# A decoder step with a mixture of experts: the expert loop written out, three places for weights, and the up-projection as three fp32r products

## The reference, cut to what matters

```
def hier_moe(x, w_rg, b_rg, w_re, b_re, w_e1, w_e3, w_e2):
    ...
    for g in range(N_GROUPS):
        a = jnp.einsum('nd,edf->nef', xf, w_e1[g])      # 1024 -> 256, per expert
        b = jnp.einsum('nd,edf->nef', xf, w_e3[g])      # 1024 -> 256, per expert
        hid = jax.nn.silu(a) * b * gates[:, g, :, None]
        y = y + jnp.einsum('nef,efd->nd', hid, w_e2[g]) # 256 -> 1024, per expert
```

## Time and profile before

| | us |
|---|---|
| median of 3 runs | 1281.07 |
| lowest and highest run | 1278.13, 1283.64 |
| span of the profiled execution, first to last instruction | 1278.4 |
| PE busy in it | 1121.3 (88%) |
| the experts, from the first gathered rows on PE to the last product | 837.1 to 1210.3 |

### The profile page before, as it was taken

One profiled execution on the slowest core, in us unless ns is written; L12 is line 12 of the kernel. 1 busy time (PEld: TensorE's weight loads), 2 busy tenths in 40 slices (PEclk: granted clock), 3 DMA queues, 4 the chain that ended last, 5 costly groups with the idle time before them and its releaser, 6 DMA issues. The chain is left out here.

```text
span 1278.4 us, 13014 instructions
## 1 busy us (share of the span) xinstructions
PE 1121.3 (88%) x4858; PEld 798.0 (62%) x4858; DVE 432.0 (34%) x993; ACT 250.8 (20%) x501; POOL 195.9 (15%) x229
## 2 busy tenths in 40 slices
PE   3999998999999999998789999279999999999800
PEld 3899997978864799855457787234444444444300
DVE  5816363055541000314521135711222221222165
ACT  4522110233220121303211033101011010110121
POOL 3301220000001221000103001412211222212100
PEclk9999999999999999999899999679999999999955
DMA  9401111231025310332061121338999999888383
GB/s 329 108 17 50 37 50 62 89 138 70 1 84 181 109 38 33 138 126 99 1 230 67 66 83 50 141 132 321 334 322 334 315 328 336 320 330 310 131 311 124
DMA packets 50743, 202.82 MB, mean 159 GB/s; under 512 B 10374, under 2 KB 19071, under 8 KB 41223
## 3 DMA queue, kind: packets, MB, share of 16 engines
q1 hardware_dynamic: 38615, 177.18, 39.4%
q0 software_dynamic: 12080, 24.98, 5.3%
HBM read 189.55 MB, written 28.36 MB: 170 GB/s over the span
## 5 line engine op out<-in xcount | busy, mean ns | idle before, releaser
L420 PE MATMUL bank<-regA_r,regW_r 128*128 128x352 f32 (+1 forms) x456 | 149.4, 328 | 0.0
L419 PE MATMUL bank<-regA_r,regW_r 128*128 128x352 f32 (+1 forms) x456 | 149.4, 328 | 0.0
L395 PE MATMUL bank<-regW,regY 128*128 128x512 f32 x256 | 114.7, 601 | 1.5 <-DVE regY L1763 1.5
L395 PE MATMUL bank<-regY 128*128 128x512 f32 x256 | 112.5, 592 | 1.5 <-DVE regY L1763 1.5
L291 POOL TENSOR_TENSOR regW_r<-regW,regW_r 128x1024 fp32r<-128x1024 f32 x19 | 47.2, 2487 | 307.7 <-ACT regW_r L285 307.7
L395 PEld LDWEIGHTS bank<-regW,regY 128*128 128x128 f32 x256 | 49.3, 193 | 64.0 <-issue 64.0
L418 PE MATMUL bank<-regY_r,regW_r 128*128 128x352 f32 (+1 forms) x264 | 88.0, 333 | 0.5 <-ACT regB L981 0.5
L395 PEld LDWEIGHTS bank<-regY 128*128 128x128 f32 x256 | 48.6, 190 | 62.4 <-issue 62.4
L419 PEld LDWEIGHTS bank<-regA_r,regW_r 128*128 128x128 f32 x456 | 86.5, 190 | 0.4
L420 PEld LDWEIGHTS bank<-regA_r,regW_r 128*128 128x128 f32 x456 | 86.0, 189 | 0.0
L1770 DVE TENSOR_TENSOR regA<-regA,bank 128x256 f32<-128x256 f32 x32 | 13.5, 421 | 213.8 <-ACT regA L1231 213.8
(11 more groups left out here) (279 smaller groups left out, 1774.9 us busy)
## 6 DMA issues: line engine op xcount, KB each, us to landing
regW<-in_we SPq DMA_DIRECT2D x16, 2048.0 KB, 9.8
regY<-in_we SPq DMA_DIRECT2D x16, 2048.0 KB, 9.2
regY<-in_we SPq DMA_DIRECT2D x16, 1024.0 KB
regW<-in_we SPq DMA_DIRECT2D x16, 1024.0 KB
regB<-expert_rows SPq DMA_DIRECT2D x12, 512.0 KB, 5.5
regW<-in_wbc SPq DMA_DIRECT2D x11, 512.0 KB, 3.5
regA<-in_kct SPq DMA_DIRECT2D x5, 1024.0 KB, 4.9
regY<-in_cache_mem_v SPq DMA_DIRECT2D x5, 1024.0 KB, 7.6
```

Of the source, the lines that this page charges most:

```text
L395: last = nc.tensor.matmul(out, lhsT, rhs, start=(k == 0), stop=(k == len(pairs) - 1))
L419: nc.tensor.matmul(out, stays[1], moves[0], start=False, stop=False)
L420: ins = nc.tensor.matmul(out, stays[0], moves[0], start=False, stop=last)
```

## The change

Five edits, all in the expert part:

1. The hardware loops over experts are gone on all engines; all 32 experts are written out. The counters of the semaphores run over all experts instead of one for each parity. On POOL the small copies of the indices ahead of each gather and scatter (`gixg`, `gixs`) and the helper `waited` are gone there; the indirect DMAs read `idx` directly, and up to four gathers are issued ahead of the first scatter instead of three.
2. The weights have three places: `regW`, `regY` and `regS`. The third is loaded for expert 2 by SP after `s_gd` (the router's last values) and after the stores of `normed_tokens`, ahead of the first gather. From then on, SP waits for `ab(e-3)` before `W13(e)` and for `yy(e-3)` before `W2(e)`.
3. `ab` is made of three fp32r products for each of the 8 blocks (low weight x high token, high weight x low token, high x high) instead of one fp32 product.
4. For this each expert's `W13` is split: ACT rounds it in 4 pieces of 128 x 1024 into `W13hi` (two places in `regB`), DVE subtracts it in 4 pieces in place. The transposed tokens are split in 2 pieces of 128 x 512 in the same way.
5. On PE the tokens of expert `e+2` are transposed where those of `e+1` were, and `xt` signals each half. Experts 0 and 1 have their weights split ahead of the loop: on ACT before the router's exponentials, on DVE after the router's last instruction.

The order on ACT for expert `e` is now: `sil(e)`, `ht(e-1)`, two pieces of `W13(e+2)`, two of the tokens of `e+2`, two more of `W13(e+2)`, `y0(e-1)`. On DVE: `hid(e)`, `xt(e+2)`, the same pieces, `y1(e-1)`.

Diff, cut to its core. The places and PE:

```
+        R13 = [(regW, regWr, 0), (regY, regYr, 0), (regS, regSr, 0)]
+        W13hi = [v3(regBr, 4096 * s, KD, 2 * FE) for s in range(2)]
...
-            def ab(s, signal, b):
-                mm_group(bank[b][:, :], [(XGT[s][:, k, :], W13[s][:, k, :]) for k in range(KD)], signal)
+            def ab(e):
+                s, w, b = e % 2, e % 3, B_AB[e % 2]
+                if e >= 2:
+                    pe.wait_ge(m_hid, e - 1)
+                for k in range(KD):
+                    if k % 4 == 0:
+                        pe.wait_ge(m_xl, 2 * e + k // 4 + 1)
+                    if k % 2 == 0:
+                        pe.wait_ge(m_wl, 4 * e + k // 2 + 1)
+                    product(bank[b][:, :], (XGThi[s][:, k, :], XGTlo[s][:, k, :]),
+                            (W13hi[s][:, k, :], W13lo[w][:, k, :]), k == 0, k == KD - 1,
+                            m_ab if k == KD - 1 else None)
...
+            def down(e):
+                pe.wait_ge(m_ht, e + 1)
+                pe.wait_ge(m_w2[e % 3], 16 * (e // 3 + 1))
+                if e >= 1:
+                    pe.wait_ge(m_yo0, e)
+                    pe.wait_ge(m_yo1, e)
+                yy(e % 2, e % 3, m_y)
+            tokens(0)
+            tokens(1)
+            for e in range(NE):
+                ab(e)
+                if e >= 1:
+                    hidden(e - 1)
+                if e + 2 < NE:
+                    tokens(e + 2)
+                if e >= 1:
+                    down(e - 1)
```

SP, whose `load` starts one DMA:

```
-            sp.wait_ge(m_ab[0], 1)
-            load(w13_flat[0], i_["we"][2, :, 0:4096], m_w[0])
-            with sp.Fori(0, NE // 2 - 2) as i:
-                for e0, s in ((1, 1), (2, 0)):
-                    sp.wait_ge(m_ab[s], i + e0)
-                    weights(w13_flat[s], 2 * i + e0 + 2, 0, 4096, m_w[s])
-                    sp.wait_ge(m_y[1 - s], i + 1)
-                    weights(w2_flat[1 - s], 2 * i + e0 + 1, 4096, 6144, m_w2[1 - s])
+            sp.wait_ge(s_gd, 1)
+            sp.wait_ge(s_xnd[0], 16 * 5)
+            sp.wait_ge(s_xnd[1], 16 * 4)
+            load(w13_flat[2], i_["we"][2, :, 0:4096], m_w[2])
+            load(w2_flat[2], i_["we"][2, :, 4096:6144], m_w2[2])
+            for e in range(3, NE):
+                sp.wait_ge(m_ab, e - 2)
+                load(w13_flat[e % 3], i_["we"][e, :, 0:4096], m_w[e % 3])
+                sp.wait_ge(m_y, e - 2)
+                load(w2_flat[e % 3], i_["we"][e, :, 4096:6144], m_w2[e % 3])
```

ACT:

```
+            for e in range(NE):
+                act.wait_ge(m_ab, e + 1)
+                sil(e % 2, B_AB[e % 2], m_sil)
+                if e >= 1:
+                    act.wait_ge(m_th, e)
+                    ht((e - 1) % 2, m_ht)
+                if e + 2 < NE:
+                    weight_hi(e + 2, 0)
+                    weight_hi(e + 2, 1)
+                    token_hi(e + 2, 0)
+                    token_hi(e + 2, 1)
+                    weight_hi(e + 2, 2)
+                    weight_hi(e + 2, 3)
+                if e >= 1:
+                    y_left(e - 1)
```

The split on DVE (the tokens' `token_hi` and `token_lo` are built alike):

```
+            def weight_lo(e, c):
+                s, w = e % 2, e % 3
+                dve.wait_ge(m_wh, 4 * e + c + 1)
+                tt(W13lo[w][:, 2 * c:2 * c + 2, :], W13[w][:, 2 * c:2 * c + 2, :],
+                   W13hi[s][:, 2 * c:2 * c + 2, :].bitcast(F32), ALU.subtract).then_inc(m_wl, 1)
```

POOL:

```
-                    g.wait_ge(m_si[s], i + 1)
-                    g.wait_ge(m_yo0[s], i + 1 + s)
-                    g.wait_ge(m_yo1[s], i + 1 + s)
-                    waited()
-                    scatter(s, gixs[s], m_sc[s])
+            for e in range(4):
+                rows_in(e)
+            for e in range(NE):
+                if e + 4 < NE:
+                    rows_in(e + 4)
+                if e >= 1:
+                    rows_out(e - 1)
```

More of the change, by code:

```diff
@@ L348, in trunk_step @@
         s_waited = sem("s_waited")
[L349 to L352, removed]
+        m_w = [sem(f"m_w{s}") for s in range(3)]
+        m_w2 = [sem(f"m_w2{s}") for s in range(3)]
         m_g = [sem("m_g0"), sem("m_g1")]
[L354 to L363, removed]
-        m_sc = [sem("m_sc0"), sem("m_sc1")]
+        m_sc = [sem("m_sc0"), sem("m_sc1")]
+        m_tx = sem("m_tx")
+        m_xt = sem("m_xt")
+        m_xh = sem("m_xh")
+        m_xl = sem("m_xl")
+        m_wh = sem("m_wh")
+        m_wl = sem("m_wl")
+        m_ab = sem("m_ab")
+        m_sil = sem("m_sil")
+        m_hid = sem("m_hid")
+        m_th = sem("m_th")
+        m_ht = sem("m_ht")
+        m_y = sem("m_y")
+        m_yo0 = sem("m_yo0")
+        m_yo1 = sem("m_yo1")
         o_go = sem("o_go")
@@ L717, in tx, with ab_plain @@
                 last.then_inc(signal, 1)
-            def ab(s, signal, b):
-                mm_group(bank[b][:, :], [(XGT[s][:, k, :], W13[s][:, k, :]) for k in range(KD)], signal)
+            def ab_plain(signal, b):
+                mm_group(bank[b][:, :], [(XGT[0][:, k, :], W13[0][:, k, :]) for k in range(KD)], signal)
+            def ab(e):
[10 more added lines that the diff above has]
+                            m_ab if k == KD - 1 else None)
             def th(s, signal):
@@ L779, in _ @@
+            tokens(0)
[8 more added lines that the diff above has]
+                    down(e - 1)
+            hidden(NE - 1)
+            down(NE - 1)
             pe.wait_ge(o_go, 1)
@@ L1223, in _, with weight_hi, token_hi @@
                     copy(rts[t % 2][:, 0:r], ps[0:LG, 0:r], sg)
+            def weight_hi(e, c):
+                s, w = e % 2, e % 3
+                if c == 0:
+                    act.wait_ge(m_w[w], 16 * (e // 3 + 1))
+                nc.scalar.activation(W13hi[s][:, 2 * c:2 * c + 2, :], W13[w][:, 2 * c:2 * c + 2, :],
+                                     ACT.Copy).then_inc(m_wh, 1)
+            def token_hi(e, q):
+                act.wait_ge(m_xt, 2 * e + q + 1)
+                nc.scalar.activation(XGThi[e % 2][:, 4 * q:4 * q + 4, :], XGT[e % 2][:, 4 * q:4 * q + 4, :],
+                                     ACT.Copy).then_inc(m_xh, 1)
+            filled(act, ("O2", NT - 1, 1))
+            for e in range(2):
+                for c in range(4):
+                    weight_hi(e, c)
             act.wait_ge(s_gd, 1)
@@ L1906, in _ @@
             g.sem_inc(o_yo, 1)
-            for s in range(2):
-                g.wait_ge(m_sc[s], 16)
             g.wait_ge(o_sc, 16)
@@ L1969, in _, with rows_in @@
-            g.wait_ge(m_tx[1], NH - 1)
-            g.tensor_copy(gixg[1][:, :], idx[:, 2 * NE - 2:2 * NE]).then_inc(m_gi[1], 1)
-            g.wait_ge(m_gi[1], NH)
-            gather(1, gixg[1], m_g[1])
-            for e in range(NE - 4, NE):
-                s, n = e % 2, e // 2
-                g.wait_ge(m_sc[s], 16 * n + 16)
-                g.tensor_copy(gixs[s][:, :], idx[:, 2 * e:2 * e + 2]).then_inc(m_si[s], 1)
-                g.wait_ge(m_si[s], n + 1)
-                g.wait_ge(m_yo0[s], n + 1 + s)
-                g.wait_ge(m_yo1[s], n + 1 + s)
-                scatter(s, gixs[s], m_sc[s])
+            def rows_in(e):
+                if e >= 2:
+                    g.wait_ge(m_tx, e - 1)
+                gather(e % 2, idx[:, 2 * e:2 * e + 2], m_g[e % 2])
@@ L1981, in _, with rows_out @@
+            def rows_out(e):
+                g.wait_ge(m_yo0, e + 1)
+                g.wait_ge(m_yo1, e + 1)
+                scatter(e % 2, idx[:, 2 * e:2 * e + 2], m_sc[e % 2])
+            for e in range(4):
+                rows_in(e)
+            for e in range(NE):
+                if e + 4 < NE:
+                    rows_in(e + 4)
+                if e >= 1:
+                    rows_out(e - 1)
+            rows_out(NE - 1)
             for s in range(2):
-                g.wait_ge(m_sc[s], 16 * (NH + 1))
+                g.wait_ge(m_sc[s], 16 * (NE // 2))
```

200 lines of the change are left out of this document (69 added, 131 removed).

## The result

The changed kernel took 1287.75 us (median of 20 runs, 1279.75 to 1297.46) beside 1282.63 for the kernel before (20 runs, 1277.64 to 1285.84). The ratio is 1.0049, with a 95% interval of 1.0028 to 1.0070: slower by half a per cent, where 3.7 us less were forecast. The profiled execution took 1286.53 us, its span is 1284.7. The runs of after scatter twice as widely as those of before, and the long ones are those at a low clock: 1297.46 us belongs to a granted clock of 0.934, 1280.58 to one of 0.945. Over the 20 runs the correlation of the two is -0.69. Part of the scatter is from ahead of the experts: there too the clock falls for longer in some of the 13 profiles (6.8 us instead of 3.4 near 589 us), and in the four with this longer fall the load of `idx` comes at 833.4 us or later, in the nine others at 831.1 or earlier.

What follows compares the result with a forecast made beforehand. PE bounds the kernel before, transfers only a tenth below; after the change a two-round ring of waits holds the loop. Start -2.3, 29 rounds x 0.0 and end -1.4 sum to -3.7: 1277.4 us against 1281.07, range 1259 to 1299.

Steps and rivals of the forecast that it cites:

- PE's work: Expert rounds: the cheaper ab takes 5.47 us instead of 6.87, so PE's own round falls from 11.39 to 9.99.
- the ring: Expert loop: chain of waits from one yy through weight loads, ACT and DVE to yy two rounds later, 22.8 us.
- the pair's landing: Expert loop: W2(e) and W13(e+1), requested together, land in 11.2 us, chosen between 9.9 and 12.0.
- ACT and DVE: Expert loop: from W13's landing through the split pieces to the end of DVE's y1, 7.8 us.
- SP's request: Expert loop: SP asks for W2 and the next W13 3.8 us after yy starts, reacting 0.35 after its end.
- the third place: Expert loop: a third weight buffer does not help, as the ring goes through the order on ACT and DVE.
- over 29 such rounds nothing is won and nothing lost: Expert loop: the ring gives 11.4 us a round against 11.39 before, so 29 rounds contribute 0.0 us.
- rival C: Expert loop: PE's clock falls in pauses ahead of yy, +0.83 us in every round, +24 in all: 1301; chance 0.17.
- The start: First experts: first tx at 839.5, behind expert 2's load, yet yy(0) ends earlier: -2.3 us (bounds -5 and +1.5).
- The end: Last expert: once the last weights are in, ab(31) runs without the ring, 1.4 us less.
- Rival D: Expert loop: W2 and W13 take 12.0 us or more to land, 11.8 a round, +8: 1289; chance 0.13.
- The rule on rings that take turns: Start: DMA engines alternate between queues by packet, so the first gather need not wait; PE starts near 838, 1.5 us earlier.

Runs made afterwards that it cites:

- the second profile: The changed kernel run once more, unchanged: 1288.52 us (10 runs), ratio 1.0058 to before; the profile is from this run.
- three ways: Changed kernel with y copies ahead of the pieces: 1265.27 us; W13 requested ahead of W2(e-1), still after yy: 1261.66; W13 requested ahead of the wait for yy: 1241.53.
- Mending both: Changed kernel with expert 2's loads held until two gathers landed, plus one 256-column constants' product on PE ahead of down(e-1): 1278.68 us, ratio 0.9971 to before.
- The held loads: Changed kernel with SP holding expert 2's loads until the first two gathers have landed: 1281.19 us, ratio 0.9985 to before.
- the small product: Changed kernel with one unread 256-column fp32 product of constants on PE ahead of down(e-1): 1281.53 us, ratio 0.9996 to before.
- the one with two products: Changed kernel with two unread fp32 products of constants (512 and 256 columns) on PE ahead of down(e-1): 1286.96 us, ratio 1.0030 to before.

## Why the prediction was wrong

- **PE's work and the ring were right.** PE's own round was forecast at 9.99 and is 10.02. The ring was forecast at 22.8 and is 22.84 (22.64 in the second profile) wherever the clock is full: the pair's landing 11.39 against 11.2 taken, ACT and DVE 7.5 against 7.8, SP's request 3.7 behind the start of `yy` against 3.8; 0.24 from `y1` to `yy`, is what the sum did not have. The 11.2 was a choice between 9.9 and 12.0, so that it came so near is in part luck. Opening or shortening it in three ways gave 18, 21 and 41 us below before. That the third place does not help was argued; no run takes it away.
- **The step that failed is "over 29 such rounds nothing is won and nothing lost".** That 0.0 priced the ring at a clock of 1.00, and the pause it makes ahead of `yy` at nothing. The pause is rival C's: four falls in each profile of after, and the rounds took 7.9 us more than before in the first and 4.2 in the second. C had the mechanism, but as all or nothing (0.83 in every round, 1301, chance 0.17); in fact some 4 of 15 pauses above 1 us bring the clock down. The place was right, and for a short fall the price: `yy` loses 1.7 us in it, against the 1.65 taken; in a long one it loses 2.7 to 3.0. Either kind makes a second ring late too, which C did not have. A share of C belonged in the forecast's own sum: a quarter of C's 24 us would have turned -3.7 into +2.
- **The start was mis-sized.** -2.3 was forecast from a first `tx` 2.4 later than before; it is 4.3 later (the gather's rows need 8.83 instead of 4.49), beyond the upper bound of 841, and the first `yy` stands 30.31 after the load of `idx` as against 30.39 before: 0. The bound had the 3 MB landed at 840.1; they landed at 841.62, and the first gather at 841.44. The remaining 0.4 us of the miss lie between the first `tx` and the end of `yy(0)`, 22.4 against 22.0: ahead of `ab(0)` stands `tx(1)`, 1.94 us at half clock, which the sum left out.
- **The end was right.** From the 30th `yy` to the last one it is 15.94 us in before and 14.57 in after: -1.37, where -1.4 was forecast.
- **Sum.** In the first trace the start gave -0.1 (for -2.3), the rounds +7.9 (for 0.0) and the end -1.4 (as forecast): the last `yy` stands 6.4 later than in before, where -3.7 was the sum, a miss of 10.1. Mending both took 9.8 us off the time.
- **Rival D** gives nearly the time that was measured (1289) but its reason is not there: at full clock the pair takes 11.4 and not 12.0, and in after DMA is at 0.78 in the very stretches that are slow.

Open is how the 9.8 us split. The held loads give 3.3 by the trace; the small product's share is then some 6.5, which contains its own price. That the falls lengthen the rings is seen in the rows of `yy` and `ab` and in the two runs with the small product, not in the one with two products. That nothing else differs between the runs of the changed kernel is not shown, as only two of them have a trace.

The rule on the clock cited with C (the Trainium skill, "TensorE: Matmul & The Clock Gate", HAM oscillation) is borne out in part: PE's waits did bring the slow clock back, but after about one pause in four and not in each tile. The rule on rings that take turns (the Trainium skill, "DMA: Bandwidth & Descriptors", Queues, rings and completion order) would, by the prediction's estimate, have had the first `tx` 1.5 us earlier than taken; the trace has it 2.1 later. From 837 to 841 us packets of both queues do move in turn, 158 and 223, as the rule says; what the estimate lacked is that none of the gather's moved in the first 4.6 us behind its issue.

## What to carry to other kernels

When PE gets faster than a ring of waits around it, its gain comes back as pauses, and pauses have a price of their own in the clock: sum the ring at the clock that a pausing PE gets, not at the full one. Before splitting operands to make a product cheaper, look where the requests for the next operands stand in the queue: here one load asked for ahead of a wait was worth 46 us, in a change that as it stood lost 5. A load that is moved ahead of a gather is paid by the gather.

## What the runs showed of the hardware

- The clock can fall after pauses of 2.00, 2.04, 2.17 and 2.39 us between dense products, and stay up through one of 3.09 in the same kernel and 3.21 in another; it is not the length of the pause alone. This pause of 3.09 did nothing to the clock, that of 2.39 cost 1.7 us:

```profile
917.70 3.67 PE L401 MATMUL bank<-regS,regA 128*128 128x512 f32 x8 [3.09 <-DVE regA L1819]
...
1079.97 5.37 PE L401 MATMUL bank<-regY,regA 128*128 128x512 f32 x8 [2.39 <-DVE regA L1819]
```

- The first fp32r product behind the fp32 ones of `yy` takes 0.79 instead of 0.40 (1003.35 above; behind the short ones of `tx`, at 853.71 in after, it takes 0.47), while its start overlaps the end of `yy` (3.67 from 1000.24), so that the switch costs next to nothing in the round (10.02 where nothing waits, against 9.99 worked out).
- Two loads asked for 0.37 us apart on one queue land one behind the other (5.24 and 3.36 us apart, 27 pairs each), yet 1 MB ahead of 2 MB puts the landing of the 2 MB back by only 1.30.
- A gather issued some 2.3 us behind a load of 2 MB and one of 1 MB on another queue has its first packet 4.2 to 4.6 us after its issue, in eight profiles, and 1.7 to 2.0 after it with no load in front, in five.
